# The context recurrence's gate products, done per head in half the array's rows instead of in block-diagonal pairs

## The chip, the cores and the metric

One core of a Trainium2 chip. The time is device microseconds of one whole execution. TensorE (PE) multiplies, VectorE (DVE) and ScalarE (ACT) work elementwise and bring results out of the eight PSUM banks, SyncE (SP) issues the transfers. Each engine takes its own instructions in the order in which they are written, and waits on semaphores for the others.

## The reference, cut to the part that matters

The program is a transformer block followed by a mixer block. The mixer's recurrence (RG-LRU) starts from states that 256 context tokens give. For them, in both directions n:

```python
def rglru(v, lp, h0):
    xc = jnp.stack([depthwise_conv(v, lp['a_conv'][0], A_CONV - 1, 0),
                    depthwise_conv(v, lp['a_conv'][1], 0, A_CONV - 1)])
    xh = xc.reshape(2, bsz, t, N_HEADS_A, HEAD_DIM)                       # 8 heads of 64
    r = jax.nn.sigmoid(jnp.einsum('nbthi,nhij->nbthj', xh, lp['a_wr'])... + lp['a_br'])
    ig = jax.nn.sigmoid(jnp.einsum('nbthi,nhij->nbthj', xh, lp['a_wi'])... + lp['a_bi'])
    log_a = -RG_C * r * jax.nn.softplus(-lp['a_lam'])
    a = jnp.exp(log_a)
    b = jnp.sqrt(-jnp.expm1(2.0 * log_a)) * (ig * xc)
    ...   # h = a * h + b along the tokens; the last h is the mixer's start
```

A head's 64 channels meet a 64x64 matrix of their own for each of the two gates r and ig. The rest of the program is attention, a state space branch, two feed-forward blocks, an embedding and the mixer proper.

## The kernel before

Everything is laid out with channels on the 128 partitions. The context's 512 recurrence channels are four tiles `ct` of 128, that is of two heads each; `KX[n][:, ct]` (128x256) holds the convolved context of direction n, `KR` and `KG` of the same shape take the gates r and ig.

All the orders are written out by hand. One Python function per engine and stage writes that engine's instructions; `tensor` calls, in this order, `glu()`, `context_rows()` (the context's projection), `ssm_rows(0)`, `context_gates()`, `ssm_rows(1)`, `ssm_rows(2)`, `ssm_rows(3)` and then `attention()`. So the context's small products stand between the large products of the state space branch's output (`ssm_rows`, four units of four results `yb`, each result twelve matmuls).

PSUM banks go round: `banks.take(use, end)` gives the next of the eight banks and notes the event that frees it; TensorE waits for the end of the use before. Results `cgt` take sixteen banks in a row, and are freed by ScalarE; results `yb` are freed by VectorE's product with `GBR` into `TMP`.

**TensorE, `context_gates` (L957).** For each ct, n and gate q one product of `GWC[:, ct, 2n+q]` (128x128, the two heads' 64x64 matrices on its diagonal, zeros beside them) and `KX[n][:, ct]`: sixteen products of 256 columns in single precision, each of which the trace shows as two records.

**ScalarE, `context` (L1719).** After a weight conversion (`WS<-RAW`) it takes sixteen sigmoids 128x256 out of the banks, with the gate's bias column; then `CKV<-LR` twice, a table load, four exponentials and four tanh for each direction, then the next weight conversion, three `CQ<-LR`, a table load, two square roots, a weight conversion.

**VectorE, `context` (L2955).** `KG = KG * KX` for each direction waits for ScalarE's last gate of that direction (L2978); then `CKV` twice, four `TMP<-PS,GBR` of `ssm_rows(1)`, the low half of a weight conversion (it waits for ScalarE's high half), six steps on `KR` and `KX`, four `TMP<-PS,GBR` of `ssm_rows(2)`, a weight conversion, `KG*KR` twice, three `CQ`, the eight scans with two copies, four `TMP<-PS,GBR` of `ssm_rows(3)`, and on to the attention's heads.

**The attention's start.** TensorE's first head products (`PS<-CKV,WS`) take banks that are long free; the next (`PS<-WS,CKV`, 24 matmuls) take banks that the `yb` results of `ssm_rows(3)` lie in, and so wait for VectorE's `TMP<-PS,GBR`.

**SyncE** loads GWC once (L3777), long ahead. The mixer proper later does its own gates (`gates`, L1165 and L1985) from a tile `GW` that holds both gates of a head side by side, in products of 64 rows.

Of the kernel before, what the change touches and what calls it, by code (L numbers as in the profile page):

```python
# [7 lines left out]
F32 = mybir.dt.float32  # L8
# [244 lines left out]
def build(nc, t, plan):  # L253
# [28 lines left out]
    def at(name, kb, shape, dt):  # L282
        return nc.alloc_sbuf_tensor_at(name, shape, dt, offset=base + int(kb * KB))
# [46 lines left out]
    ZG = at("ZG", 128, [128, 2, 4, 1024], F32R)  # L330
    CX = at("CX", 184, [128, 8, 256], F32)
    VK = at("VK", 96, [128, 4, 264], F32)
    GWC = at("GWC", 112, [128, 4, 4, 128], F32)
    KX, KR, KG = ([at(f"{name}{n}", 56 + 4 * j + 12 * n, [128, 4, 256], F32) for n in range(2)]
                  for j, name in enumerate(("KX", "KR", "KG")))
    GBR = at("GBR", 80, [128, 2, 1024], F32)
# [121 lines left out]
    def bank(*use):  # L458
        return PS[:, banks.slot.get(use, 0), :]
# [98 lines left out]
    def tensor(e):  # L558
# [9 lines left out]
        def mms(items):  # L568
            for out, l, r, first, last in items:
                done = d.matmul(out, l, r, start=first, stop=last)  # L570
            return done
# [385 lines left out]
        def context_gates():  # L957
            for ct in range(4):
                for n in range(2):
                    for q in range(2):  # L960
                        use = ("cgt", ct, n, q)
                        banks.take(use, (ac, *use))
                        e.wait_ge(dma("gwc")("gwc"), ve("kx", n, ct), *banks.free(use))
                        mms([(bank(*use)[:, 0:256], GWC[:, ct, 2 * n + q, :], KX[n][:, ct], True, True)]).then_inc(*mm.inc(*use))

        def ssm_rows(j):
            u = w.take()
# [380 lines left out]
    def scalar(e):  # L1348
        d, w, side = e.do, Units(forms), iter(())

        def act(out, x, f, bias=0.0, scale=1.0):
            return d.activation(out, x, f, bias=bias, scale=scale)  # L1352
# [366 lines left out]
        def context():  # L1719
            def split(name, dst, i0, n):  # L1720
                for k in range(n):
                    e.wait_ge(dma(f"lr{i0 + k}")("lr"), ve("kx", 1, 3), mm("cgt", 3, 1, 1))
                    if name == "q":
                        e.wait_ge(ve("ckv", 1))
                    act(dst[:, 0, k, :], LR[i0 + k][:], ACT.Copy).then_inc(*ac.inc("c" + name, k))

            for ct in range(4):
                u = w.take()
                e.wait_ge(mm("vk", ct))
                act(VK[:, ct, 3:259], bank("vk", ct)[:, 0:256], ACT.Copy).then_inc(*ac.inc("vk", ct))  # L1730
                release(u)
            ssm_rows(0)
            for ct in range(4):
                for n in range(2):
                    for q, (dst, name) in enumerate(((KR, "a_br"), (KG, "a_bi"))):
                        e.wait_ge(mm("cgt", ct, n, q), mm("glu", 3, 1))
                        act(dst[n][:, ct], bank("cgt", ct, n, q)[:, 0:256], ACT.Sigmoid, bias=col(name, 4 * n + ct)).then_inc(
                            *ac.inc("cgt", ct, n, q))
            split("kv", CKV, 1, 2)
            for n in range(2):  # L1740
                for ct in range(4):
                    e.wait_ge(ve("kg", n))
                    act(KX[n][:, ct], KR[n][:, ct], ACT.Exp, scale=GL[:, 4 * n + ct:4 * n + ct + 1]).then_inc(*ac.inc("kexp", n, ct))
                for ct in range(4):
                    e.wait_ge(ac("kexp", n, 3))
                    act(KR[n][:, ct], KR[n][:, ct], ACT.Tanh, scale=GL[:, 8 + 4 * n + ct:8 + 4 * n + ct + 1]).then_inc(
                        *ac.inc("ktanh", n, ct))
            ssm_rows(1)
            split("q", CQ, 3, 3)
            for n in range(2):  # L1750
                e.wait_ge(ve("kv3", n))
                act(KR[n][:], KR[n][:], ACT.Sqrt, scale=-1.0).then_inc(*ac.inc("ksq", n))
            ssm_rows(2)
            ssm_rows(3)
# [477 lines left out]
    def vector(e):  # L2232
# [722 lines left out]
        def context():  # L2955
# [19 lines left out]
                release(u)  # L2975
            ssm_rows(0)
            for n in range(2):
                e.wait_ge(ac("cgt", 3, n, 1), mm("cgt", 3, n, 1))  # L2978
                tt(KG[n][:], KG[n][:], KX[n][:], ALU.mult).then_inc(*ve.inc("kg", n))
            split("kv", CKV, 1, 2)  # L2980
            ssm_rows(1)
# [667 lines left out]
    def sync(e):  # L3649
# [124 lines left out]
        e.wait_ge(dma("lat")("q"), mm("zt", 3, 1), mm("gb", 7, 1))  # L3774
        load_latent(0)
        d.dma_start(CS0[64:128, :], t["rope"]).then_inc(*dma("cs0").inc("cs"))
        d.dma_start(GWC[:], t["gw"].rearrange("c p (a n) -> p c a n", a=4)).then_inc(*dma("gwc").inc("gwc"))  # L3777
        for i in (1, 2, 3):
            load_latent(i)
        e.wait_ge(mm("glu", 3, 1))  # L3780
# [195 lines left out]
def pack(i):  # L3976
# [58 lines left out]
    for n in ("c_ln_g", "c_ln_b", "c_pw_b", "d_scale"):  # L4035
        c[n] = cols_of(i[n + "_2"][0])
    c["d_b"] = i["d_b_2"][0].T
    gw, gq = np.zeros((4, 128, 4, 128), np.float32), np.zeros((4, 128, 3, 128), np.float32)
    for ct in range(4):
        for n in range(2):  # L4040
            for q, name in enumerate(("a_wr_2", "a_wi_2")):
                for e in range(2):
                    gw[ct, 64 * e:64 * e + 64, 2 * n + q, 64 * e:64 * e + 64] = i[name][0, n, 2 * ct + e]
                    o = 64 * (e ^ q)
                    gq[ct, 64 * e:64 * e + 64, n, o:o + 64] = i[name][0, n, 2 * ct + e]
        gq[ct, :, 2] = i["d_w_2"][0, ct]
# [28 lines left out]
    for a, kind in w:  # L4075
# [5 lines left out]
            tiles.append(a)  # L4081
            entries.append((kind, "ring", (n,), 0))
    arrays = {
        "gw": gw.reshape(4, 128, 512),
        "gq": gq.reshape(4, 128, 384),
        "cnt": np.tile(cnt.reshape(1, 320), (128, 1)),
        "ctxT": i["ctx_2"][0].T.reshape(8, 128, 256),
# [27 lines left out]
```

## Time and profile before

| | us |
|---|---|
| median of 3 runs (lowest to highest) | 3148.76 (3148.34 to 3150.01) |
| time of the profiled execution | 3148.84 |
| its span in the trace | 3147.0 |
| TensorE busy / VectorE busy / ScalarE busy | 3099.2 / 2360.8 / 1254.2 |
| the sixteen context gate products on TensorE | 1144.74 to 1151.46 |
| the sixteen sigmoids on ScalarE, up to the next instruction | 1145.96 to 1152.22 |

Times inside the execution count from the span's start. The stage that the change touches lies at about 1145 to 1152 of 3147. In a timeline, a row is a run of like instructions on one engine: start, length up to the end of the last, and in brackets how long the engine had been idle and what ended the wait. The granted clock is given as a share of TensorE's full clock.

### The profile page before, as it was taken

How to read it: one execution, taken by the hardware profiler on the slowest of the kernel's cores; microseconds unless marked ns; L12 is line 12 of the kernel's file. 1: busy time of each engine (PE TensorE's matmuls, PEld its weight loads, DVE VectorE, ACT ScalarE, POOL GpSimd, SP SyncE). 2: the span in 40 equal slices, each digit the busy share in tenths (PEclk: the TensorE clock that was granted, in tenths of full speed). 3: DMA queues.
4: the chain of work that ended last, by engine and by line, in shares of the span. 5: the costliest groups of instructions: out<-in, count | busy, mean ns of one | idle time of the engine just before them, and what ended most of it. 6: DMA issues, size and time to landing. Idle time of an engine off the chain costs nothing.

```text
span 3147.0 us, 38018 instructions
## 1 busy us (share of the span) xinstructions
PE 3099.2 (98%) x14840; PEld 2531.3 (80%) x14840; DVE 2360.8 (75%) x4053; ACT 1254.2 (40%) x1952; POOL 90.2 (3%) x113
## 2 busy tenths in 40 slices
PE   8999999999999999999999999999999999999998
PEld 6887888877988888888878888888777688788887
DVE  6777767778859678778598767667798689789736
ACT  4233323335242456656243223223365534534414
POOL 0000000000000002332000000000000000000000
PEclk9999999999999999999999999999999999999999
DMA  3222212213333450003211111111111311122242
GB/s 131 74 74 76 78 61 67 68 67 128 104 95 134 142 192 26 14 21 137 99 54 55 53 54 53 54 47 54 67 54 52 114 70 70 41 76 101 80 167 74
DMA packets 89249, 250.15 MB, mean 79 GB/s; under 512 B 8560, under 2 KB 24816, under 8 KB 87536
## 3 DMA queue, kind: packets, MB, share of 16 engines
q1 hardware_dynamic: 89072, 247.73, 22.8%
q8 instruction: 119, 1.95, 0.2%
q14 instruction: 58, 0.48, 0.0%
HBM read 203.65 MB, written 44.04 MB: 79 GB/s over the span
## 4 chain that ended last, share of the span: by engine, by line
PE 90%; DVE 6%; ACT 3%; issue 1%; DMA 0%; POOL 0%; DVEq 0%; SPq 0%; POOLq 0%; ACTq 0%
PE PS L570 88%; PE PS L575 2%; DVE X L2245 1%; DVE WS L2237 1%; DVE XS L2245 1%; DVE HELD L2299 1%; DVE X L2237 1%; ACT XS L1352 0%; DVE XSf L2237 0%; ACT XSf L1352 0%; DMA RAW<-in_W 0%; ACT WS L1352 0%; ACT TMP L1352 0%; DVE TMP L2237 0%; DVE HELD L2237 0%
## 5 line engine op out<-in xcount | busy, mean ns | idle before, releaser
L570 PE MATMUL PS<-XS,WS 128*128 128x512 f32 (+1 forms) x6480 | 1512.2, 390 | 20.6 <-DVE XS L2237 9.4
L570 PEld LDWEIGHTS PS<-XS,WS 128*128 128x128 f32 x6480 | 1207.5, 188 | 297.8 <-issue 26.9
L570 PE MATMUL PS<-HS,WS 128*128 128x512 f32 x2208 | 512.6, 391 | 3.1 <-DVE TMP L2237 2.7
L570 PEld LDWEIGHTS PS<-HS,WS 128*128 128x128 f32 x2208 | 415.2, 188 | 93.6 <-DVE TMP L2237 3.5
L2237 DVE TENSOR_TENSOR WS<-RAW,WS 128x512 fp32r<-128x512 f32 (+1 forms) x398 | 347.2, 881 | 173.1 <-ACT WS L1352 172.5
L1352 ACT ACTIVATE WS<-RAW 128x512 fp32r<-128x512 f32 (+1 forms) x398 | 307.7, 779 | 401.2 <-PE PS L570 350.1
L2237 DVE TENSOR_TENSOR X<-PS,X 128x512 f32<-128x512 f32 x272 | 184.3, 689 | 101.7 <-PE PS L570 101.7
L2237 DVE TENSOR_TENSOR TMP<-TMP,PS 128x512 f32<-128x512 f32 x304 | 203.7, 683 | 61.2 <-PE PS L570 58.4
L570 PE MATMUL PS<-T,WS 128*128 128x512 f32 x960 | 230.6, 389 | 0.0
L570 PEld LDWEIGHTS PS<-T,WS 128*128 128x128 f32 x960 | 180.2, 188 | 37.4
L1352 ACT ACTIVATE TMP<-PS 128x512 f32<-128x512 f32 x144 | 85.0, 596 | 290.5 <-PE PS L570 273.8
L2245 DVE SCALAR_TENSOR_TENSOR CV<-UU,COL,CV 128x1024 f32<-128x1024 f32 x120 | 154.0, 1284 | 3.4
L1352 ACT ACTIVATE HS<-TMP 128x512 fp32r<-128x512 f32 x88 | 55.6, 632 | 211.4 <-DVE TMP L2245 197.2
L2237 DVE TENSOR_TENSOR PT<-PS,PT 128x512 fp32r<-128x512 f32 x128 | 81.7, 679 | 33.7 <-ACT PT L1352 32.3
L570 PE MATMUL PS<-T1h_ln,WS 128*128 128x512 f32 x320 | 105.0, 389 | 0.0
L570 PE MATMUL PS<-KH,QH 128*128 128x512 f32 x384 | 104.1, 406 | 0.2 <-DVE QH L2237 0.2
L1352 ACT ACTIVATE PT<-PS 128x512 fp32r<-128x512 f32 x128 | 69.5, 595 | 59.0 <-PE PS L575 57.7
L1352 ACT ACTIVATE TMP<-TMP 128x512 f32<-128x512 f32 x80 | 50.6, 632 | 101.4 <-DVE TMP L2237 101.4
L2237 DVE TENSOR_TENSOR HS<-TMP,HS 128x512 fp32r<-128x512 f32 x88 | 60.6, 689 | 32.4 <-ACT HS L1352 32.2
L570 PE MATMUL PS<-MH,WS 128*128 128x512 f32 x256 | 80.4, 393 | 0.0
L3050 DVE TENSOR_REDUCE COLB<-PS 128x1 f32<-128x1024 f32 x64 | 77.8, 1215 | 0.4
L1352 ACT ACT_TABLE_LOAD x56 | 71.8, 1283 | 15.1 <-DVE GG L2237 10.7
(337 smaller groups left out, 3663.6 us busy)
## 6 DMA issues: line engine op xcount, KB each, us to landing
RAW<-in_W SPq DMA_DIRECT2D x263, 512.0 KB, 3.3
RAWX<-in_W SPq DMA_DIRECT2D x30, 512.0 KB, 3.2
DC<-TMP SPq DMA_DIRECT2D x32, 256.0 KB, 2.1
X<-in_xT SPq DMA_DIRECT2D x8, 512.0 KB, 8.7
DX<-X SPq DMA_DIRECT2D x2, 2048.0 KB, 9.1
DCZ<-CA SPq DMA_DIRECT2D x8, 512.0 KB, 4.3
DGA<-TMP SPq DMA_DIRECT2D x16, 256.0 KB, 2.1
DGB<-TMP SPq DMA_DIRECT2D x16, 256.0 KB, 2.8
```

The source lines that it names most:

```text
L570: done = d.matmul(out, l, r, start=first, stop=last)
L575: done = d.transpose(out, x, idn)
L1352: return d.activation(out, x, f, bias=bias, scale=scale)
L2237: return d.tensor_tensor(out, a, b, op)
L2245: return d.scalar_tensor_tensor(out=out, in0=a, scalar=s, in1=b, op0=op0, op1=op1)
L2299: d.reciprocal(out[:, 0:width], tmp("rs", name, h)[:, 0:width]).then_inc(*ve.inc("rs", name, h))
L3050: d.tensor_reduce(mx, PS[:, 2 + 2 * (n % 2):4 + 2 * (n % 2), :], AX.XY, ALU.max).then_inc(*ve.inc("mx", n))
```

## The change

The weights of the gates now come from the array that the mixer proper uses: for a head e of tile ct, its 64 rows hold both 64x64 matrices side by side, r's at columns 64e and ig's at columns 64(1-e). A product takes 64 rows (one head, p) and gives both gates of that head as 128 rows of a bank. There are still sixteen products of 256 columns. ScalarE now takes each bank in two quarters of 64x256, and each (ct, n) pair of banks in the order r of p=0, r of p=1, ig of p=0, ig of p=1; ig comes from the other 64 rows of the bank than those that it goes to. A bank is free after its ig quarter. The old array `gw` is gone, and GWC is half as large.

```diff
-    GWC = at("GWC", 112, [128, 4, 4, 128], F32)
+    GWC = at("GWC", 112, [128, 4, 2, 128], F32)
...
             for ct in range(4):
                 for n in range(2):
-                    for q in range(2):
-                        use = ("cgt", ct, n, q)
-                        banks.take(use, (ac, *use))
+                    for p in range(2):
+                        use, rows = ("cgt", ct, n, p), slice(64 * p, 64 * p + 64)
+                        banks.take(use, (ac, "cgi", ct, n, p))
                         e.wait_ge(dma("gwc")("gwc"), ve("kx", n, ct), *banks.free(use))
-                        mms([(bank(*use)[:, 0:256], GWC[:, ct, 2 * n + q, :], KX[n][:, ct], True, True)]).then_inc(*mm.inc(*use))
+                        mms([(bank(*use)[:, 0:256], GWC[rows, ct, n, :], KX[n][rows, ct], True, True)]).then_inc(*mm.inc(*use))
...
-                    for q, (dst, name) in enumerate(((KR, "a_br"), (KG, "a_bi"))):
-                        e.wait_ge(mm("cgt", ct, n, q), mm("glu", 3, 1))
-                        act(dst[n][:, ct], bank("cgt", ct, n, q)[:, 0:256], ACT.Sigmoid, bias=col(name, 4 * n + ct)).then_inc(
-                            *ac.inc("cgt", ct, n, q))
+                    for what, dst, name in (("cgr", KR, "a_br"), ("cgi", KG, "a_bi")):
+                        for p in range(2):
+                            rows, at_ = slice(64 * p, 64 * p + 64), 64 * p if what == "cgr" else 64 - 64 * p
+                            e.wait_ge(mm("cgt", ct, n, p), mm("glu", 3, 1))
+                            act(dst[n][rows, ct], bank("cgt", ct, n, p)[at_:at_ + 64, 0:256], ACT.Sigmoid,
+                                bias=col(name, 4 * n + ct)[rows]).then_inc(*ac.inc(what, ct, n, p))
...
-                e.wait_ge(ac("cgt", 3, n, 1), mm("cgt", 3, n, 1))
+                e.wait_ge(ac("cgi", 3, n, 1), mm("cgt", 3, n, 1))
...
-        d.dma_start(GWC[:], t["gw"].rearrange("c p (a n) -> p c a n", a=4)).then_inc(*dma("gwc").inc("gwc"))
+        d.dma_start(GWC[:], t["gq"].rearrange("c p (a n) -> p c a n", a=3)[:, :, 0:2]).then_inc(*dma("gwc").inc("gwc"))
```

ScalarE's order at the gates of tile ct = 0, before (`KR_109`, `KG_111` are r and ig of direction 0, `KR_110`, `KG_112` of direction 1):

```order
L1352 ACTIVATE WS<-RAW 128x1024 [waits matmul_done,dma_unit1]
L1352 ACTIVATE KR_109<-PS,COL 128x256 [waits matmul_done]
L1352 ACTIVATE KG_111<-PS,COL 128x256 [waits matmul_done]
L1352 ACTIVATE KR_110<-PS,COL 128x256 [waits matmul_done]
L1352 ACTIVATE KG_112<-PS,COL 128x256 [waits matmul_done]
```

And the same place now:

```order
L1352 ACTIVATE WS<-RAW 128x1024 [waits matmul_done,dma_unit1]
L1352 ACTIVATE KR_109<-PS,COL 64x256 [waits matmul_done] x2
L1352 ACTIVATE KG_111<-PS,COL 64x256 x2
L1352 ACTIVATE KR_110<-PS,COL 64x256 [waits matmul_done] x2
L1352 ACTIVATE KG_112<-PS,COL 64x256 x2
```

Sixteen instructions of 128 rows have become thirty-two of 64 rows; nothing else on ScalarE has another place.

TensorE's order from the last four gate products into `ssm_rows(1)`, which reads the same in both kernels, since only the rows of the operands differ (`KX_107`, `KX_108` are the two directions):

```order
L570 MATMUL PS<-KX_107,GWC 128x256 [waits activation_done] x2
L570 MATMUL PS<-KX_108,GWC 128x256 [waits activation_done] x2
L570 MATMUL PS<-ZG,WS 128x512 [waits activation_done,weight_lo_done,weight_hi_done]
L570 MATMUL PS<-ZG,WS 128x512 x11
L570 MATMUL PS<-ZG,WS 128x512 [waits activation_done]
```

The first eight gate products take banks that older results held; the last eight each wait for ScalarE to free one of the first eight's, and the eight results of `ssm_rows(1)` and `ssm_rows(2)` each for one of the last eight's. The event they wait for has moved to the ig quarter of that bank.

VectorE's order behind the gates, which also reads the same in both:

```order
L2237 TENSOR_TENSOR WS<-RAW,WS 128x1024 [waits weight_hi_done]
L2237 TENSOR_TENSOR KG_111<-KG_111,KX_107 128x1024 [waits matmul_done,activation_done]
L2237 TENSOR_TENSOR KG_112<-KG_112,KX_108 128x1024 [waits matmul_done,activation_done]
L2237 TENSOR_TENSOR CKV<-LR_115,CKV 128x1024 [waits activation_done]
L2237 TENSOR_TENSOR CKV<-LR_116,CKV 128x1024 [waits activation_done]
L2237 TENSOR_TENSOR TMP<-PS,GBR 128x512 [waits dma_gbr0,matmul_done]
```

The wait of `KG_112` has moved from the sixteenth full sigmoid to the thirty-second quarter, that of `KG_111` from the fourteenth to the twenty-eighth.

## Rows read from the trace of the kernel before

**Rows 1.** the page: busy us, share and count by engine; chain by engine

```profile
PE 3099.2 (98%) x14840; PEld 2531.3 (80%) x14840; DVE 2360.8 (75%) x4053; ACT 1254.2 (40%) x1952; POOL 90.2 (3%) x113
...
PE 90%; DVE 6%; ACT 3%; issue 1%; DMA 0%; POOL 0%; DVEq 0%; SPq 0%; POOLq 0%; ACTq 0%
```

**Rows 2.** timeline of TensorE, 1136 to 1215: start, length, instruction, [idle before, releaser]

```profile
1144.74 7.07 PE L570 MATMUL PS<-KX,GWC 128*128 128x256 f32 x32
1151.46 33.00 PE L570 MATMUL PS<-ZG,WS 128*128 128x512 f32 x144
1184.30 2.88 PE L570 MATMUL PS<-CKV,WS 128*128 128x512 f32 x12
1187.55 3.10 PE L570 MATMUL PS<-WS,CKV 128*128 128x256 f32 x24 [0.37 <-DVE TMP L2237]
1191.06 4.34 PE L570 MATMUL PS<-CQ,WS 128*128 128x512 f32 x18 [0.42 <-DVE KH L2237]
...
1198.50 2.98 PE L570 MATMUL PS<-KH,QH 128*128 128x512 f32 x12 [0.22 <-DVE QH L2237]
```

**Rows 3.** timeline of ScalarE in the same stretch, same columns

```profile
1145.96 0.46 ACT L1352 ACTIVATE KR<-PS,COL 128x256 f32<-128x256 f32 x1
1146.32 0.46 ACT L1352 ACTIVATE KG<-PS,COL 128x256 f32<-128x256 f32 x1
...
1151.84 0.48 ACT L1352 ACTIVATE KG<-PS,COL 128x256 f32<-128x256 f32 x1
1152.22 2.00 ACT L1352 ACTIVATE CKV<-LR 128x1024 fp32r<-128x1024 f32 x2
...
1160.62 1.71 ACT L1352 ACTIVATE KR<-KR,COLB 128x256 f32<-128x256 f32 x4
1162.80 1.06 ACT L1352 ACTIVATE WS<-RAW 128x1024 fp32r<-128x1024 f32 x1 [0.47 <-PE PS L570]
```

**Rows 4.** timeline of VectorE in the same stretch (TENSOR_TENSOR and others)

```profile
1151.49 2.36 DVE L2237 TENSOR_TENSOR KG<-KG,KX 128x1024 f32<-128x1024 f32 x2 [4.11 <-ACT KG L1352]
...
1163.89 1.23 DVE L2237 TENSOR_TENSOR WS<-RAW,WS 128x1024 fp32r<-128x1024 f32 x1 [0.46 <-ACT WS L1352]
...
1171.28 1.88 DVE L2237 TENSOR_TENSOR TMP<-PS,GBR 128x512 f32<-128x512 f32 x3
1173.62 0.69 DVE L2237 TENSOR_TENSOR TMP<-PS,GBR 128x512 f32<-128x512 f32 x1 [0.46 <-PE PS L570]
1174.77 1.23 DVE L2237 TENSOR_TENSOR WS<-RAW,WS 128x1024 fp32r<-128x1024 f32 x1 [0.46 <-ACT WS L1352]
...
1186.71 2.48 DVE L2237 TENSOR_TENSOR TMP<-PS,GBR 128x512 f32<-128x512 f32 x4
```

**Rows 5.** timeline of ScalarE, 2570 to 2620: the mixer's gates in quarters

```profile
2590.87 2.81 ACT L1352 ACTIVATE GG<-PS,COL 64x512 f32<-64x512 f32 x4
```

**Rows 6.** groups by line and form: busy us, mean ns

```profile
L1352 ACT ACTIVATE GG<-PS,COL 64x512 f32<-64x512 f32 x32 | 21.9, 685 | 0.8
```

**Rows 7.** timeline of TensorE, 2570 to 2620: the mixer's half-array pairs

```profile
2589.62 1.99 PE L570 MATMUL PS<-XC,GW 64*128 64x512 f32 x8
2591.54 22.05 PE L570 MATMUL PS<-XS,WS 128*128 128x512 f32 x96
```

**Rows 8.** timeline of TensorE, 1120 to 1145

```profile
1132.11 12.79 PE L570 MATMUL PS<-ZG,WS 128*128 128x512 f32 x48 [2.36 <-issue]
```

**Rows 9.** 2 us windows: busy PE, PEld, DVE, ACT, POOL; then clock, DMA share, GB/s

```profile
1132.00:1134.00 2.00, 1.89 (x8) 1.56 (x9) 1.89 (x6) 1.01 (x1) 0.00 (x0) 0.89 0.62 231
1134.00:1136.00 2.00, 2.00 (x6) 1.63 (x5) 1.89 (x5) 0.92 (x2) 0.00 (x0) 0.50 0.23 88
1136.00:1138.00 2.00, 2.00 (x8) 1.55 (x8) 1.93 (x4) 0.19 (x1) 0.00 (x0) 0.75 0.18 25
```

**Rows 10.** the tile GWC: its load and how long it took to land

```profile
L3777 SPq DMA_DIRECT2D GWC<-in_gw x1: 587/587/587, 1091.9 to 1091.9; - x1
...
DMA to landing us min/median/max: 8.8/8.8/8.8
```

More of the change, by code:

```diff
@@ L4037, in pack @@
     c["d_b"] = i["d_b_2"][0].T
-    gw, gq = np.zeros((4, 128, 4, 128), np.float32), np.zeros((4, 128, 3, 128), np.float32)
+    gq = np.zeros((4, 128, 3, 128), np.float32)
     for ct in range(4):
@@ L4042, in pack @@
                 for e in range(2):
-                    gw[ct, 64 * e:64 * e + 64, 2 * n + q, 64 * e:64 * e + 64] = i[name][0, n, 2 * ct + e]
                     o = 64 * (e ^ q)
@@ L4083, in pack @@
     arrays = {
-        "gw": gw.reshape(4, 128, 512),
         "gq": gq.reshape(4, 128, 384),
```

## The prediction

> **What bounds the kernel now.** I read the page first: TensorE is busy for 98% of the span, and the chain that ended last is 90% TensorE and 6% VectorE [rows 1]. So a change matters if it moves TensorE, or if it moves one of the few places where TensorE waits. Then the timeline of TensorE around the change: the gate products start at 1144.74, the next instruction at 1151.46, so the sixteen products hold TensorE for 6.72 us, 0.42 each; then come twelve `yb` results without a gap until 1184.30, the first head products until 1187.18 (1184.30 + 2.88), a wait of 0.37 us for VectorE's `TMP`, and smaller waits of 0.42 and 0.22 us up to the scores at 1198.50 [rows 2]. The first of these waits says that at 1187 VectorE, not TensorE, is last. What VectorE does before it is in its own timeline: four short waits (4.11, 0.46, 0.46, 0.46 us), and none from 1174.77 to 1186.71, a full queue [rows 4]. Its longest, 4.11 us, is for ScalarE's gates. ScalarE's timeline: sixteen sigmoids from 1145.96 to 1152.22, 6.26 us, then work without a gap up to a wait of 0.47 us at 1162.80 [rows 3]. So the chain to watch is ScalarE's gates, its work up to `WS<-RAW`, VectorE's queue, `TMP` at 1186.71, TensorE at 1187.55.
>
> **TensorE's products.** The same number of instructions and columns, on 64 rows instead of 128. The trace has this form in the mixer: eight records of 64x512 start at 2589.62, the next instruction at 2591.54, 1.92 us [rows 7]. A record of 256 columns holds TensorE for 0.21 us (6.72/32), one of 512 columns for twice that, 0.42; eight in sequence would be 3.4 us, four 1.7. So two heads do run beside each other, and the context's products would take 6.72/2 = 3.4 us if nothing held them: a gain of 3.3 us at the most.
>
> **ScalarE's quarters.** Here is the cost: 32 instructions for 16, each of as many columns. A full sigmoid lasts 0.46 to 0.48 us, but in a queue the next starts 0.36 us after it (1146.32 - 1145.96): they overlap by 0.1 [rows 3]. The mixer's quarters, which alternate between the halves of the rows as the new ones do, do not: four last 2.81 us [rows 5] at 0.685 each [rows 6], so they start (2.81 - 0.685)/3 = 0.71 us apart, 0.02 more than one lasts. I take the same for 256 columns: 0.47 + 0.02 = 0.49 us apart. The bounds: below, 0.36 apart, if they overlap as the full ones do; above, the mixer's 0.71, for twice the columns. I take the length from the row with the same 256 columns and the missing overlap from the row with the same order of halves, the same bias column and the same PSUM source. Sum: 32 x 0.49 = 15.7 us instead of 6.26, ScalarE is 9.4 us late behind the gates (5.3 at 0.36; 16.5 at 0.71, which only a quarter whose length does not depend on its columns would give).
>
> The Trainium skill, "ScalarE: Activation LUTs", section "What ACT_TABLE_LOAD costs", gives an activation with a bias column about 280 ns + 0.833 ns a column and says that back-to-back ones overlap by about 93 ns; that makes an estimate of 0.40 us apart, 12.8 us for 32. The mixer's rows agree with its duration (0.707 against 0.685) and not with the overlap where the halves alternate.
>
> **TensorE behind the gates.** Its pairs no longer wait for TensorE's own pace but for banks. The first eight products find theirs free; product 8 (the ninth) needs the ig quarter of product 0, and so on. The first `yb` of `ssm_rows(1)` takes the bank of the ninth product, whose ig quarter is the nineteenth of ScalarE's: 1145.96 + 19 x 0.49 = 1155.3, against 1151.46 before. So TensorE, instead of gaining 3.3 us, is 3.8 us late here, and arrives at the wait of 1187.55 at 1187.18 + 3.8 = 1191.0. What counts is when VectorE arrives there.
>
> **VectorE's queue.** ScalarE's lag of 9.4 reaches its `WS<-RAW` less the gap before it: tanh ended at 1160.62 + 1.71 = 1162.33 and the conversion could start 0.09 earlier, by the overlap of queued rows, instead of 1162.80 [rows 3]. That gives back 0.56: the conversion is 8.8 us late. VectorE's low half waits for it (the 0.46 at 1163.89 says so) and is 8.8 late too, 1172.7; slack that VectorE has before it doesn't help, because this wait comes behind it. From there VectorE runs in a full queue to 1171.28, now 1180.1. The fourth `TMP` no longer waits for TensorE (the 0.46 at 1173.62, with a 0.08 overlap: 0.54 back), nor the conversion behind it for ScalarE (0.46 at 1174.77, again 0.54) [rows 4]; ScalarE's own one can start once the second square root is done, 1180.2 + 1.0, and ends at 1182.3, VectorE asks for it at 1182.6. What is left is 8.85 - 1.08 = 7.8 us. `TMP` of 1186.71 starts at 1194.5, TensorE's 1187.55 becomes 1195.3. TensorE has arrived 4.3 us before. **TensorE is 7.8 us late from here on**, and so is all that it feeds.
>
> **Other edits.** GWC is loaded half as large and at the same place of SyncE's queue; it was issued at 1091.9 and landed 8.8 us later, 44 us before its use [rows 10]: nothing, and without that cover at most those few us. VectorE's `KG` waits for another count, costed above. SyncE's loads for the `yb` products are issued behind the `TMP` results of two rows earlier and move with them.
>
> **The clock.** Before `ssm_rows(0)` TensorE was idle for 2.36 us [rows 8], and in the 2 us windows behind it the granted clock is 0.89, 0.50 and 0.75 of full [rows 9]: from 2.4 to 1.2 GHz and back. What is lost at full clock is (0.11 + 0.50 + 0.25) x 2 = 1.7 us. The new wait before 1195.3 is 4.3 us of idleness, longer than that one, so I expect the clock to fall there too. TensorE has 0.42 + 0.22 = 0.64 us of slack up to the scores [rows 2]: cost 1.7 - 0.64, about 1.0 us; bounds 0 (it does not fall) and about 3 (twice the loss, if it stays down for longer). It will likely fall among the gates as well; there TensorE is not last and it costs nothing.
>
> **The sum.** 3148.84 (the profiled execution's own time, 0.08 above the median, which I leave at that) + 7.8 + 1.0 = 3157.6 us. Behind the scores TensorE is bound by its own work again, so I take nothing off; waits for transfers are 0% of the chain [rows 1].
>
> The Trainium skill, "TensorEngine Tiling (Array Packing)", section "PSUM Bottleneck", speaks against the change: "Tiling speeds up TensorE but not PSUM evacuation". It puts no price on it; the price here is the 9.4 us of the rows.
>
> **The rivals.**
> A. The forecast: quarters 0.47 to 0.51 apart. ScalarE +8.8 to +10.1, lag 7.1 to 8.5, clock 0 to 3: 3156 to 3160. Chance 0.78. For it: the mixer's rows, the same code with other sizes.
> B. The other side, not slower by what can be measured: the quarters overlap, 0.36 to 0.41 apart. ScalarE +5.3 to +6.9, lag 3.6 to 5.2, no clock loss up to the full 1.0: 3152.4 to 3155.0. It decides at a spacing of (6.3 - 1.0 + 1.64 + 6.26)/32 = 0.41 us with the clock's 1.0, 0.44 without: below that the change is not slower by 0.2%. For it: the full sigmoids' 0.36; against it: the mixer's rows [rows 5, 6]. Chance 0.16. The overlap that the Trainium skill states in "ScalarE: Activation LUTs", section "What ACT_TABLE_LOAD costs", would lead here, with 0.40.
> C. TensorE's gain comes through: 3148.8 - 3.3 = 3145.5. It needs ScalarE's lag to vanish into slack before 1187, and the wait of 0.37 there says that there is none; TensorE would have to be last, and even then its own banks hold it. Chance 0.03.
> D. The halves do not run side by side here, although they do in the mixer: TensorE takes 6.7 us as before. Then nothing changes in the sum, since ScalarE sets the pace. It has no time of its own and lies in A and B.
> E. Something behind adds to it (quarters longer than the full sigmoids, or a longer stretch at half clock): above 3160.5, chance 0.03.
>
> **How the numbers follow.** The likeliest case gives 3157.6. The range from 3152.8 to 3160.5 takes in A with both bounds of the clock and most of B. A measurement of this kernel can tell about 0.2%, 6.3 us, from no change: slower by more than that means above 3155.1. A and E, less its lowest corner: 0.77; within: B and that corner, 0.20; faster: C, 0.03.
>
> **What would show it.** ScalarE's `KR` and `KG` rows as 64x256, 32 of them, 0.49 apart, up to about 1161.7; if 0.36 to 0.40 apart, B. TensorE's first `yb` row behind the gates at 1155.3, with waits for ScalarE among the `KX,GWC` rows. VectorE's wait for `KG` grown from 4.1 to about 12 us. `TMP` at 1194.5 and behind it TensorE's row at 1195.3 with a wait of about 4 us for `TMP`. The granted clock below 1 in windows among the gates and behind 1195. The forecast is wrong if VectorE arrives at `TMP` with less lag than 6 us, or if TensorE's waits further behind shrink in return.

## The result and the profile after

| | median | lowest to highest | runs |
|---|---|---|---|
| before | 3148.56 us | 3147.21 to 3150.22 | 8 |
| after the change | 3156.9 us | 3156.45 to 3160.17 | 8 |

The ratio is 1.0028, with a 95% interval of 1.0018 to 1.0038: the change makes the kernel 8.3 us slower, forecast were 8.8. The profiled execution of the changed kernel took 3160.17 us, the longest of its eight; its span is 3158.4 us, and part of what it has over the median lies outside the changed stage (below).

The page after it, the lines that answer to [rows 1] (busy us, share and count by engine; the chain's walk back covers only 64% of the span here, so its shares are not compared):

```profile
span 3158.4 us, 38034 instructions
...
PE 3107.5 (98%) x14840; PEld 2535.2 (80%) x14840; DVE 2360.2 (75%) x4053; ACT 1263.1 (40%) x1968; POOL 90.4 (3%) x113
```

ScalarE has sixteen instructions more and is busy for 9 us more; VectorE's work is the same.

TensorE's timeline, 1130 to 1225, which answers to [rows 2]:

```profile
1144.48 1.13 PE L570 MATMUL PS<-KX,GWC 64*128 64x256 f32 x8
1145.88 2.40 PE L570 MATMUL PS<-KX,GWC 64*128 64x256 f32 x8 [0.27 <-DVE TMP L2239]
1148.54 1.19 PE L570 MATMUL PS<-KX,GWC 64*128 64x256 f32 x4 [0.26 <-ACT KG L1352]
1150.52 1.71 PE L570 MATMUL PS<-KX,GWC 64*128 64x256 f32 x4 [0.79 <-ACT KG L1352]
...
1156.55 34.49 PE L570 MATMUL PS<-ZG,WS 128*128 128x512 f32 x144 [0.37 <-ACT KG L1352]
1190.88 2.88 PE L570 MATMUL PS<-CKV,WS 128*128 128x512 f32 x12
1196.52 4.60 PE L570 MATMUL PS<-WS,CKV 128*128 128x256 f32 x24 [2.76 <-DVE TMP L2239]
1200.96 4.25 PE L570 MATMUL PS<-CQ,WS 128*128 128x512 f32 x18
...
1207.92 2.91 PE L570 MATMUL PS<-KH,QH 128*128 128x512 f32 x12
```

The first four products (eight records) take 1.13 us, side by side; four full ones took 4 x 0.42 = 1.7. The next four wait for banks that VectorE's `TMP` frees. From the ninth on TensorE waits for ScalarE's ig quarters, as the rows `<-ACT KG` say, and the `yb` products start 12.1 us behind the first gate product (1156.55 - 1144.48), where it was 6.7. And before the second group of head products TensorE waits 2.76 us for VectorE's `TMP`.

ScalarE's timeline in the same stretch, which answers to [rows 3]:

```profile
1147.04 0.95 ACT L1352 ACTIVATE KR<-PS,COL 64x256 f32<-64x256 f32 x2
1148.02 0.96 ACT L1352 ACTIVATE KG<-PS,COL 64x256 f32<-64x256 f32 x2
...
1161.88 0.97 ACT L1352 ACTIVATE KG<-PS,COL 64x256 f32<-64x256 f32 x2
1162.88 2.02 ACT L1352 ACTIVATE CKV<-LR 128x1024 fp32r<-128x1024 f32 x2
...
1172.90 1.04 ACT L1352 ACTIVATE WS<-RAW 128x1024 fp32r<-128x1024 f32 x1
```

Thirty-two quarters from 1147.04 to 1162.88: 15.84 us, 0.495 apart (0.49 was forecast), and 0.469 is the middle length of a `KR` quarter. `WS<-RAW` has no wait before it any more.

VectorE's timeline, which answers to [rows 4]:

```profile
1160.90 1.23 DVE L2239 TENSOR_TENSOR KG<-KG,KX 128x1024 f32<-128x1024 f32 x1 [12.24 <-ACT KG L1352]
1162.88 1.23 DVE L2239 TENSOR_TENSOR KG<-KG,KX 128x1024 f32<-128x1024 f32 x1 [0.76 <-ACT KG L1352]
...
1173.98 1.23 DVE L2239 TENSOR_TENSOR WS<-RAW,WS 128x1024 fp32r<-128x1024 f32 x1 [3.97 <-ACT WS L1352]
...
1181.37 2.48 DVE L2239 TENSOR_TENSOR TMP<-PS,GBR 128x512 f32<-128x512 f32 x4
1183.76 1.21 DVE L2239 TENSOR_TENSOR WS<-RAW,WS 128x1024 fp32r<-128x1024 f32 x1
...
1195.68 2.48 DVE L2239 TENSOR_TENSOR TMP<-PS,GBR 128x512 f32<-128x512 f32 x4
```

The wait for `KG` has grown from 4.11 to 12.24 us; behind the wait for `WS` at 1173.98 the queue is full up to `TMP`, and the two waits of 0.46 that stood there are gone. The kernel before also had three waits of VectorE for `yb` results ahead of `WS` (0.58, 2.03 and 2.03 us, from 1156 to 1163), which [rows 4] leaves out; now one of 1.15 us is left of them, at 1169.32.

**Measuring by events.** Two executions reach this stage at times up to 1.7 us apart (the first sigmoid at 1145.96 before, 1147.04 after), so I compare distances between events of one execution: from the start of the first `KR<-PS` to that of the last row `TMP<-PS,GBR`, and from there to the first score (`KH,QH`). The column "ScalarE" is the time from the first sigmoid to `CKV`. All times in us, from the timelines; "waits" is TensorE's before `WS,CKV`.

| kernel | ScalarE | sigmoid to TMP | waits | TMP to score | sigmoid to score |
|---|---|---|---|---|---|
| before | 6.26 | 40.75 | 0.37 | 11.79 | 52.54 |
| after | 15.84 | 48.64 | 2.76 | 12.24 | 60.88 |
| e1_quarters | 15.79 | 48.60 | 4.83 | 12.76 | 61.36 |
| e2_grouped | 13.52 | 46.45 | 0.37 | 11.79 | 58.24 |
| e3_tiles64 | 5.70 | 39.74 | 0.37 | 11.78 | 51.52 |
| e4_noscan | 15.79 | 43.63 | none | 13.44 | 57.07 |
| e5_fill_head | 15.79 | 48.61 | 0.16 | 11.79 | 60.40 |
| e6_noscan_fill | 15.87 | 43.70 | none | 11.79 | 55.49 |
| e7_half | 10.77 | 43.57 | 2.29 | 11.79 | 55.36 |
| e8_fill_both | 15.80 | 48.62 | 1.62 | 11.79 | 60.41 |
| e9_grouped_fill | 13.55 | 46.36 | none | 11.80 | 58.16 |
| e10_change (the changed kernel again) | 15.82 | 48.63 | 1.97 | 11.78 | 60.41 |
| e11_grouped (e2_grouped again) | 13.55 | 47.38 | 0.37 | 11.80 | 59.18 |

In the two profiled executions the difference of the spans, 11.4 us, falls into three parts: 1.08 ahead of the first sigmoid, 8.34 from there to the first score, and 2.0 behind it (1948.5 us from the first score to the end before, 1950.5 after). In the outer two both kernels do the same, and the clock fell once more often in each of them in the changed kernel's execution: ahead of the stage at 754 and 1095 (before: at 1133.6), behind it at 1484. The tail shows what such a fall costs. All executions have a fall in their last 20 us. In the seven profiled ones without another behind the first score (before, e2, e3, e4, e6, e9, e10) the rest takes 1948.5 to 1948.7 us, whatever the kernel; in the five with one 1949.8 to 1950.5, in e7_half with two 1951.9.

### The profile page after: what moved, and what is told of

The parts are those of the page before. It is cut to its first block, busy times and chain, and to the rows that moved or that the text cites. A ratio compares the mean times of both kernels' runs of the same rounds, so it can differ in the third digit from the quotient of the medians.

```text
span 3158.4 us, 38034 instructions
## 1 busy us (share of the span) xinstructions
PE 3107.5 (98%) x14840; PEld 2535.2 (80%) x14840; DVE 2360.2 (75%) x4053; ACT 1263.1 (40%) x1968; POOL 90.4 (3%) x113
## 4 chain that ended last, share of the span: by engine, by line
PE 55%; DVE 5%; ACT 3%; issue 1%; DMA 0%; POOL 0%; DVEq 0%; POOLq 0%; ACTq 0%; SPq 0%
PE PS L570 54%; PE PS L575 2%; DVE WS L2239 1%; DVE HELD L2301 0%; DVE X L2239 0%; DVE X L2247 0%; DVE KX L2247 0%; DVE XS L2247 0%; ACT KR L1352 0%; DVE TMP L2239 0%; ACT XS L1352 0%; DVE XSf L2239 0%; ACT KG L1352 0%; DVE TMP L2247 0%; ACT L1352 0%
## 5 line engine op out<-in xcount | busy, mean ns | idle before, releaser
L3052 DVE TENSOR_REDUCE COLB<-PS 128x1 f32<-128x1024 f32 x64 | 77.8, 1215 | 0.5
```

Source lines behind the costliest of these rows:

```text
L3052: d.tensor_reduce(mx, PS[:, 2 + 2 * (n % 2):4 + 2 * (n % 2), :], AX.XY, ALU.max).then_inc(*ve.inc("mx", n))
```

## The experiments

All changes are against the changed kernel, unless it says otherwise. e1 to e4 shared a chip with runs of the kernel before, whose median was 3148.62 us there; for e5 to e8 it was 3148.57, for e9 to e11 3148.43. A ratio's interval of 0.001 to each side is 3 us. So the intervals do not separate kernels whose medians are one or two us apart; where I compare such kernels, the argument rests on the distances in the traces, of one execution each.

### e1_quarters: the quarters alone

```diff
 # against the kernel before
                     for q, (dst, name) in enumerate(((KR, "a_br"), (KG, "a_bi"))):
-                        e.wait_ge(mm("cgt", ct, n, q), mm("glu", 3, 1))
-                        act(dst[n][:, ct], bank("cgt", ct, n, q)[:, 0:256], ACT.Sigmoid, ...)
+                        for p in range(2):
+                            rows = slice(64 * p, 64 * p + 64)
+                            e.wait_ge(mm("cgt", ct, n, q), mm("glu", 3, 1))
+                            act(dst[n][rows, ct], bank("cgt", ct, n, q)[rows, 0:256], ACT.Sigmoid, ...)
```

> The kernel before with one part of the change alone: TensorE's sixteen full products stay, ScalarE takes each bank in two quarters of 64x256 instead of one sigmoid of 128x256. My theory (ScalarE's 32 quarters, 0.49 us apart because the halves of the rows alternate, set the end): the quarters take 15.8 us as in the changed kernel, VectorE's TMP before the head products comes 7.5 to 9 us late, and the time is that of the changed kernel within 1 us, 3156 to 3158 us. Rival 1 (the half-array products or the order of their banks are what costs): about 3148.6 us. Rival 2 (it costs more than in the changed kernel, since TensorE also keeps its 3.3 us): 3160 us.

Measured: 3158.9 us (3157.26 to 3160.27, 6 runs), ratio 1.0031 (1.0019 to 1.0042). ScalarE 15.79 us, `TMP` at 48.60: as in the changed kernel to 0.05 us, without any half-array product. Rival 1 falls: the quarters alone make the whole lag at `TMP`, without the new products, rows and banks. Rival 2 (3160 us) has the median almost as near as my range has, but not its mechanism: TensorE's first `yb` starts 8.99 us behind the first sigmoid (9.51 in the changed kernel), and TensorE waits 4.83 us for `TMP`, so it is not last. The median is 0.9 us above the range of my theory; 0.5 of it is the longer way from `TMP` to the score (12.76), behind a wait of 4.83 us, and the rest I can't tell from the spread of the runs.

### e2_grouped: another order of the quarters

```diff
 # the events that free the banks and release KG follow the new order
+                for what, dst, name, p in (("cgr", KR, "a_br", 0), ("cgi", KG, "a_bi", 1), ("cgr", KR, "a_br", 1), ("cgi", KG, "a_bi", 0)):
+                    for n in range(2):
```

> The changed kernel with ScalarE's quarters in another order: for each tile both directions' r of head 0, then both ig of head 1 (same rows of PSUM, other rows of SBUF), both r of head 1 (other rows of PSUM, same of SBUF), both ig of head 0. Every second quarter uses the same rows as the one before it. My theory (a quarter cannot overlap the one before it if it changes the half of the rows): 16 starts 0.36 us and 16 starts 0.49 us behind the one before, 13.6 us in all instead of 15.8, and the time falls by about 2.2 us, to 3154.5 us. Rival (a quarter of 64 rows never overlaps, whatever comes before it): 0.49 everywhere, time as the changed kernel, 3157 us. The trace also tells whether a change of the PSUM rows alone or of the SBUF rows alone is enough.

Measured: 3157.47 us (3154.51 to 3158.46, 10 runs), ratio 1.0027 (1.0018 to 1.0037). ScalarE's timeline, in which each row is two quarters on the same rows:

```profile
1148.44 0.83 ACT L1352 ACTIVATE KR<-PS,COL 64x256 f32<-64x256 f32 x2
1149.30 0.83 ACT L1352 ACTIVATE KG<-PS,COL 64x256 f32<-64x256 f32 x2
1150.15 0.83 ACT L1352 ACTIVATE KR<-PS,COL 64x256 f32<-64x256 f32 x2
1151.01 0.82 ACT L1352 ACTIVATE KG<-PS,COL 64x256 f32<-64x256 f32 x2
```

A row lasts 0.83, and a quarter 0.46, so the second starts 0.36 behind the first; the next row starts 0.49 behind that (0.855 from row to row). So 64 rows do overlap, as full ones do, if the one before used the same half, and the rival falls. From a `KR` row to a `KG` row the half of SBUF changes (with the bias column's) and that of PSUM doesn't, from `KG` to `KR` it is the other way round: either alone costs the overlap. (The tile changes too from `KR` to `KG`, but the full sigmoids alternate in the same way and overlap.) `TMP` came 2.19 us earlier (46.45), as forecast. But the median is 3157.47 and not 3154.5, no better than the changed kernel's. Two things could hide the 2.2 us: what happens elsewhere in the execution, or TensorE. Its banks come free later in this order (the first `yb` starts 9.98 us behind the first sigmoid, 9.51 in the changed kernel), its clock is halved for ten us there, and it takes 34.22 us for the `yb` products. The next three runs are on that.

### e9_grouped_fill, e10_change, e11_grouped: where the reordering's 2.2 us went

e10_change is the changed kernel, e11_grouped is e2_grouped, and e9_grouped_fill is e2_grouped with this:

```diff
-                        mms([(bank(*use)[:, 0:256], GWC[rows, ct, n, :], KX[n][rows, ct], True, True)]).then_inc(*mm.inc(*use))
+                        mms([(bank(*use)[:, 0:256], GWC[rows, ct, n, :], KX[n][rows, ct], True, True)] * 3).then_inc(*mm.inc(*use))
...
+                if p == 0:
+                    mms(group3(PS[:, m, :], pairs))
                 mms(group3(PS[:, m, :], pairs)).then_inc(*mm.inc(*use))
```

> e2_grouped with TensorE's gate products issued three times and the first two head products twice, as in e8_fill_both. In e2_grouped the first score came 2.64 us earlier than in the changed kernel's profile, but the median time did not fall. My theory: in e2_grouped TensorE, at half clock among the gates, arrives together with VectorE at the head products, so that in many executions it is last; with the clock kept up this goes: from the first sigmoid to the first score 58.2 us, and the median 2 us or more below that of the changed kernel on the same chip. Rival: the medians of e2_grouped and the changed kernel differ by what happens elsewhere, and the filling changes nothing: this kernel within 0.5 us of e2_grouped.

> The changed kernel itself, for comparison on one chip with the two others of this call. All theories: 3156.5 to 3158 us, 48.6 us from the first sigmoid to TMP.

> e2_grouped again, beside the changed kernel on one chip. My theory: its median is 0.5 to 2 us below the changed kernel's, less than the 2.2 us by which TMP comes earlier, since TensorE is then as late as VectorE. Rival (the order of the quarters gains nothing at all): the same median as the changed kernel within 0.5 us.

Measured on one chip: e10_change 3157.54 us (3156.32 to 3158.65, 8 runs), ratio 1.0027 (1.0017 to 1.0037); e11_grouped 3156.99 us (3155.39 to 3158.41, 10 runs), ratio 1.0027 (1.0018 to 1.0037); e9_grouped_fill 3155.42 us (3154.02 to 3157.68, 11 runs), ratio 1.0022 (1.0013 to 1.0031). TensorE's timeline of e11_grouped:

```profile
1155.70 35.12 PE L570 MATMUL PS<-ZG,WS 128*128 128x512 f32 x144 [1.44 <-ACT KG L1352]
```

and of e9_grouped_fill:

```profile
1156.43 32.93 PE L570 MATMUL PS<-ZG,WS 128*128 128x512 f32 x144
```

With the clock kept up the reordering is worth 2.1 us in the median and 2.25 in the stage (58.16 against 60.41, which e8_fill_both, the changed kernel with the same filling, needs too); without it, 0.55 in the median and 1.2 in the stage. So TensorE at half clock had taken part of the gain: in e11_grouped VectorE's `TMP` is itself late (47.38), since the `yb` results come late (VectorE waits 0.38 us for one and then 0.46 for ScalarE's `WS`, and in e9_grouped_fill for neither). The intervals of the three overlap, and 0.55 lies so near the rival's 0.5 that the medians do not separate the two; it is the stage's times in the traces that tell the cause. They do not explain all: in e2_grouped's own profiled execution the stage had gained 2.64 us, in spite of the fall, and the median had not. Even so, ScalarE's rearranged quarters with the filling are 7 us slower than the kernel before.

### e3_tiles64: one gate of both heads in one bank

```diff
 # against the kernel before, with the changed kernel's weights
+                        for p in range(2):
+                            rows, o = slice(64 * p, 64 * p + 64), 64 * (p ^ q)
+                            items.append((bank(*use)[rows, 0:256], GWC[rows, ct, n, o:o + 64], KX[n][rows, ct], True, True))
```

> The changed kernel's weights, but each product split into 64 rows by 64 columns of the array, so that a bank holds one gate of both heads and ScalarE again takes sixteen full sigmoids of 128x256; 32 products instead of 16. My theory: two tiles with other rows and other columns run beside each other, TensorE's products take some 3.4 us instead of 6.7 if the banks let them, ScalarE 0.36 apart takes 5.8 us instead of 6.3; VectorE, which is last at the head products, comes only 0.5 to 2 us earlier: 3146.5 to 3148.3 us. Rival (tiles of 64x64 run one after another): TensorE holds 6.7 us or more for them and the time is that of the kernel before, 3148.6 us, or up to 3 us more.

Measured: 3149.27 us (3147.25 to 3151.18, 11 runs), ratio 1.0001 (0.9992 to 1.001): no change that can be measured. TensorE's timeline:

```profile
1143.14 7.21 PE L570 MATMUL PS<-KX,GWC 64*64 64x256 f32 x64
1150.28 32.93 PE L570 MATMUL PS<-ZG,WS 128*128 128x512 f32 x144
```

Sixty-four records in 7.14 us: 0.11 each, so two do run beside each other. My 3.4 us was wrong: I had halved the time of the sixteen products and forgotten that there are now thirty-two. Two at a time they need as long as before. With ScalarE at 0.36 apart `TMP` comes 1.0 us earlier, as forecast, and so does the first score, but the medians don't show it: 3149.27 lies above my 3146.5 to 3148.3 and where the rival had it, though the rival's reason (one tile after another) is not what the trace shows. It also says that ScalarE's full tiles, given back, take away the whole loss.

### e4_noscan: VectorE's queue shortened

```diff
-                for ct in range(4):
-                    y, x, b = (v[n][:, ct, ::-1] if n else v[n][:, ct] for v in (KR, KX, KG))
-                    scan(y, x, b, 0.0).then_inc(*ve.inc("kscan", n, ct))
```

> The changed kernel without VectorE's eight context scans (4.9 us of its queue between the gates and the TMP results that the head products wait for); the part left out is the recurrence over the context tokens, the final states are taken from what the tiles hold. My theory (VectorE's queue is last there, TensorE arrives 3 to 4.3 us before it): TMP comes 4.9 us earlier, TensorE's wait goes, the clock does not fall there, and the time falls by 3.5 to 5.5 us, to 3151.5 to 3153.5 us; 3.8 us of TensorE's own lag from the gates stay. Rival (TensorE's own stalls among the gates make the loss): the time stays at 3157 us.

Measured: 3155.21 us (3153.34 to 3157.14, 10 runs), ratio 1.0019 (1.001 to 1.0029); the profiled execution took 3153.34. `TMP` came 5.0 us earlier (43.63), TensorE's wait is gone, and the first score came 3.81 us earlier. So VectorE was last in the changed kernel, and TensorE's own lag is next behind it. The way from `TMP` to the score is 13.44 us, 1.65 more than before: TensorE starts `WS,CKV` 3.59 us behind `TMP`, where VectorE would let it start after 0.84, and makes up 1.1 of these 2.75 us because it has no waits any more (9.85 us from there to the score, 10.95 before). The stage's 3.81 us lie in the forecast of 3.5 to 5.5; the median fell by 1.7 only. The profiled execution is the fastest of the ten, and where the other 2.1 us of the median went its trace doesn't show. The clock, in 2 us windows of e4_noscan (busy PE, PEld, DVE, ACT, POOL; then granted clock):

```profile
1148.00:1150.00 2.00, 1.21 (x6) 0.62 (x5) 0.00 (x0) 1.90 (x5) 0.00 (x0) 1.00 1.07 272
1150.00:1152.00 2.00, 1.63 (x6) 0.91 (x5) 0.00 (x0) 1.90 (x5) 0.00 (x0) 0.51 0.90 285
...
1158.00:1160.00 2.00, 2.00 (x6) 1.52 (x6) 0.24 (x1) 1.90 (x5) 0.00 (x0) 0.50 0.00 0
1160.00:1162.00 2.00, 2.00 (x10) 1.62 (x9) 1.24 (x2) 1.90 (x5) 0.00 (x0) 0.93 0.02 4
```

Behind the first gates, where TensorE is busy for 1.21 of 2 us and on half of its rows, the clock is 1.2 GHz for ten us, almost five of them in `yb` products (from 1155.43 on), whose twelve then take 35.2 us instead of 32.9.

### e6_noscan_fill: the same with TensorE kept busy among the gates

```diff
 # against e4_noscan
-                        mms([(bank(*use)[:, 0:256], GWC[rows, ct, n, :], KX[n][rows, ct], True, True)]).then_inc(*mm.inc(*use))
+                        mms([(bank(*use)[:, 0:256], GWC[rows, ct, n, :], KX[n][rows, ct], True, True)] * 3).then_inc(*mm.inc(*use))
```

> The kernel of e4_noscan (no context scans) with each of TensorE's context gate products issued three times, the last one counting. In e4_noscan TensorE was last at the head products, and its granted clock was 0.5 from 1150 to 1160. My theory: the clock fell because TensorE had too little to do among the gates, and that cost e4_noscan what VectorE's earlier arrival had gained; with the filling the clock stays at 1, the twelve yb results take 33 us instead of 35, and the time falls by 1.5 to 2 us against e4_noscan's 3155.2, to about 3153.4 us. Rival: the clock falls in the same way (it is not a matter of how busy TensorE is), and the time stays or grows.

Measured: 3152.74 us (3151.09 to 3154.25, 11 runs), ratio 1.0012 (1.0004 to 1.0021), 2.5 us below e4_noscan. TensorE's timeline:

```profile
1145.04 11.19 PE L570 MATMUL PS<-KX,GWC 64*128 64x256 f32 x96
1156.19 32.92 PE L570 MATMUL PS<-ZG,WS 128*128 128x512 f32 x144
```

Three times the work, no fall of the clock among the gates, `yb` in 32.92 us, the first score 1.58 us earlier than in e4_noscan. The clock fell because TensorE had too little to do, and where TensorE is last that costs 1.6 us. The medians' 2.5 us are more than the 1.5 to 2 forecast and more than the stage shows; the two ran on different chips and their intervals overlap.

### e5_fill_head and e8_fill_both: what the clock costs the changed kernel

```diff
+                if p == 0:
+                    mms(group3(PS[:, m, :], pairs))
                 mms(group3(PS[:, m, :], pairs)).then_inc(*mm.inc(*use))
```

> The changed kernel with TensorE's first two head products issued twice (the second time they start the sum anew, the result is the same): 2.9 us of work in the time in which TensorE waits for VectorE's TMP. My theory of the clock: without the long wait the granted clock does not fall behind the head products' wait, and from the first of the four TMP results to the first score it takes the 11.8 us of the kernel before instead of 12.2 to 12.8; TMP itself comes at the same time; total 0.4 to 1.0 us less than the changed kernel, which is near what the runs can resolve. Rival: the clock falls there anyway, or falls without a cost: no change; or TensorE becomes last with the added work, up to 0.5 us more.

> The changed kernel with both fillings: gate products three times, first head products twice. My theory: no fall of the clock from 1145 to 1210; TMP still 48.6 us behind the first sigmoid, since ScalarE and VectorE set it; first score 11.8 to 12.2 us behind TMP; total within 1 us of e5_fill_head. So the clock's fall among the gates costs the changed kernel nothing there. Rival (part of the loss is TensorE at half clock among the gates): 1.5 to 2 us less than e5_fill_head.

Measured: e5_fill_head 3156.96 us (3156.68 to 3158.4, 9 runs), ratio 1.0026 (1.0016 to 1.0036); e8_fill_both, with e6's tripled gate products as well, 3157.79 us (3157.07 to 3159.1, 6 runs), ratio 1.0028 (1.0017 to 1.0039). In both `TMP` is where it was, 48.6, and from `TMP` to the score it takes 11.79 us, as before the change. The changed kernel's own windows there:

```profile
1194.00:1196.00 2.00, 0.00 (x0) 0.00 (x0) 1.97 (x5) 0.00 (x0) 0.00 (x0) 1.00 0.00 0
1196.00:1198.00 2.00, 1.48 (x10) 1.51 (x11) 2.00 (x4) 0.00 (x0) 0.00 (x0) 0.86 0.40 147
1198.00:1200.00 2.00, 2.00 (x12) 2.00 (x11) 1.90 (x3) 1.70 (x3) 0.00 (x0) 0.50 0.90 221
1200.00:1202.00 2.00, 2.00 (x11) 1.83 (x11) 1.30 (x3) 1.95 (x5) 0.00 (x0) 0.79 1.07 371
```

So the fall behind the wait is there, it is brought about by the wait, and it costs 12.24 - 11.79 = 0.45 us in this execution (0.97 in e1_quarters, where the wait is 4.83 us). In e10_change, the same kernel in another execution, the wait was 1.97 us, no fall followed, and the way to the score took 11.78: the term is there in some executions and not in others. The time does not show such an amount: the changed kernel's medians are 3156.9 and 3157.54 us, e5_fill_head's is 3156.96 and not 0.4 to 1.0 less, e8_fill_both's 3157.79. That e8 is no faster than e5 fits the other part: among the gates the fall costs the changed kernel nothing, since TensorE has a wait of 2.76 us to give. Where that wait is gone, as in e11_grouped and e4_noscan, it costs. (In e5 and e8 the clock stayed up behind a wait of 0.16 and 1.62 us.)

### e7_half: half the dose

```diff
 # against e1_quarters
-                        for p in range(2):
-                            rows = slice(64 * p, 64 * p + 64)
+                        for p in range(2 - q):
+                            rows = slice(64 * p, 64 * p + 64) if q == 0 else slice(0, 128)
```

> As e1_quarters (full products), but only r is taken in quarters, ig in one full sigmoid: 16 quarters and 8 full ones. By the rows: 16 x 0.49 + 8 x 0.36 to 0.43 = 10.8 to 11.3 us on ScalarE, 4.5 to 5 us more than before. My theory says that the first 1.64 us of such a lag disappear in gaps before VectorE's queue is full, and the rest reaches TensorE one to one: from the first sigmoid to TMP 43.7 to 44.2 us (40.75 before, 48.6 with 32 quarters), total 3151.5 to 3152.5 us with no fall of the clock. Rival (the loss is in proportion to ScalarE's extra time, 7.9 of 9.5): TMP at 44.5 to 45 us, total 3152.5 to 3153.5.

Measured: 3152.36 us (3151.59 to 3155.25, 11 runs), ratio 1.0013 (1.0004 to 1.0022). ScalarE took 10.77 us, 4.51 more than before; `TMP` stood at 43.57, 2.82 more; both lie just under their ranges, and the median is in mine. The clock fell neither among the gates nor behind the wait of 2.29 us. The 1.64 us of gaps that the prediction took off give 4.51 - 1.64 = 2.87; in proportion (7.89 of 9.58) it would be 3.7. With the full dose: 9.58 - 1.64 = 7.94, measured 7.89. Between them, in e2_grouped, ScalarE took 7.26 us more than before: 7.26 - 1.64 = 5.62, measured 5.70. The gaps are eaten first, then it is one to one. The medians alone could not have told this from the proportion; the distance to `TMP` does.

## Why the prediction was right

**TensorE's products.** Two heads side by side, and no gain, because banks hold them: both right. The stall was put at 3.8 us of lag; measured from the first sigmoid, the first `yb` comes 9.51 us behind it (1156.55 - 1147.04) against 5.50 before, 4.0 us of lag.

**ScalarE's quarters.** 0.49 us forecast, 0.495 measured; +9.4 forecast, +9.58 measured. This was the term that decided, and that it was not 0.40 or less hung on the mixer's rows alone. The full sigmoids were partly held by TensorE themselves (0.36 us apart up to the ninth, 0.43 from there on, against its 0.42 a product); the 6.26 us count both, so the sum is not touched. e2_grouped shows what is behind it, a change of half in either memory. The rule of the Trainium skill ("ScalarE: Activation LUTs", section "What ACT_TABLE_LOAD costs") that back-to-back activations overlap holds here for quarters on the same rows (0.46 long, 0.36 apart, about the 93 ns it states) and not for those that change the half (0.469 long, 0.495 apart).

**VectorE's queue.** Lag 7.8 forecast, 7.89 measured; e4_noscan shows that it is what TensorE waits for, e7_half that the gaps add up as worked out. The waits of the trace, 12.24 us for `KG` and those that vanished, are the forecast's. I had counted four waits of VectorE in the kernel before and overlooked three for `yb` results, of 0.58, 2.03 and 2.03 us. They lie ahead of the wait for `WS`, which comes last, so the sum stands as it is.

**The clock.** Behind the wait for `TMP` it fell in one profiled execution of the changed kernel and not in the other (e10_change). Its price was 0.45 us and nothing, where I put 1.0: this term of the sum was two or more times too large, within its bounds. One reason is the slack up to the scores, which I had as 0.64 us from TensorE's idle times; e4_noscan, without waits there, shows 1.1 (9.85 us instead of 10.95), and 1.7 - 1.1 would have been 0.6. The wait was 2.76 us and not 4.3, because TensorE itself was slower: I let the fall among the gates cost nothing, which is true for the end, but it took 1.5 us of TensorE's slack (`yb` in 34.49 us instead of 33.0). And that the clock fell behind the wait at all was in part luck, because waits of this size do not bring a fall each time. Ahead of `ssm_rows(0)` TensorE was idle for 2.33 to 2.51 us in eight of the thirteen profiled executions; the clock fell behind it in five (12.8 us for the `yb` row, as in [rows 8]) and not in three (e1, e3 and e7), of which e3_tiles64 shows

```profile
1132.05 11.16 PE L570 MATMUL PS<-ZG,WS 128*128 128x512 f32 x48 [2.39 <-issue]
```

Behind the wait for `TMP` it fell after 4.83 and 2.76 us and not after 2.29, 1.97 and 1.62.

**The sum.** 8.34 us from the first sigmoid to the first score, which is 7.89 + 0.45 (7.87 in e10_change), and 8.3 between the medians. That these agree to 0.1 us is partly chance: beside e10_change, on another chip, the medians lie 9.1 us apart. The forecast's 8.8 is 7.8 and 1.0, the stage's 8.34 is 7.89 and 0.45. Behind the score nothing was given back, as the tails of 1948.5 to 1948.7 us show. Rival B fell with the 0.495 us of the changed kernel's own rows, rival C with TensorE's wait for `TMP`.

"TensorEngine Tiling (Array Packing)", section "PSUM Bottleneck", of the Trainium skill says that tiling speeds up TensorE and not the taking out of PSUM. The traces agree with both parts (the first four products take 1.13 us instead of 1.7) and go further: here taking out got slower, by 9.58 us, for the 3.3 that could have been gained.

What stays open: how much of the spread of a kernel's runs (3.7 us in the changed one) is falls of the clock elsewhere. The profiled executions fit that, by their tails, and so do the mean granted clocks of the changed kernel's eight runs: 0.995 in the two longest, 0.996 or 0.997 in the others. But no run tested it. It is also open why the medians of e2_grouped and e4_noscan gained so much less than their traces. Nor did any version here beat the kernel before by what can be measured.

## What to carry to other kernels

Before splitting a result over more banks or rows, count the instructions that take it out and look up how far apart they start, not how long they last: here splitting each in two doubled that time, and alternating between the halves of the memory added more than a third to it (0.36 to 0.49 us). An engine that is 40% busy can still be the one that sets the end, if its work stands ahead of another engine's full queue; follow the waits in the stage, and take off only the gaps that lie on the chain of last waits. And if an engine is made to wait, look at who gets slower by idling: here TensorE's clock.

## What the runs showed of the hardware

- ScalarE: an activation that reads another half of PSUM's partitions, or writes another half of SBUF's (and takes its bias column from there), than the one before starts 0.02 us after its end; else 0.1 us before its end (64x256: 0.495 and 0.36 apart).
- TensorE's clock among the gates was at half for ten us in all six profiled executions with the half-array products issued once (the changed kernel, e2, e4, e5, e10, e11), although none of TensorE's waits there is longer than 0.79 us in the changed kernel. It stayed up with the same products issued three times (e6, e8, e9), with full products (before, e1, e7) and with 64x64 tiles (e3). The busy time of a window does not tell these apart: in e1_quarters it is 1.42 of 2 us at full clock, in the changed kernel 2.00 and then 1.47 in the windows up to the fall. What does is not tested. Half-array products use half of the rows, but two of them also run in less time than two full ones (a row of 1.19 us in each 1.98 at full clock, against 2 x 0.70 in e1_quarters), so TensorE also had less to do.

In e1_quarters:

```profile
1150.00:1152.00 2.00, 1.42 (x5) 0.59 (x4) 0.00 (x0) 1.90 (x5) 0.00 (x0) 1.00 0.92 331
```

In the changed kernel:

```profile
1146.00:1148.00 2.00, 2.00 (x8) 1.03 (x8) 2.00 (x4) 1.89 (x3) 0.00 (x0) 1.00 0.94 346
1148.00:1150.00 2.00, 1.47 (x6) 0.59 (x4) 0.66 (x1) 1.88 (x5) 0.00 (x0) 0.92 1.04 287
1150.00:1152.00 2.00, 1.48 (x4) 0.99 (x4) 0.00 (x0) 1.90 (x5) 0.00 (x0) 0.50 0.94 201
```

- TensorE's idle time of 2.33 to 2.51 us ahead of `ssm_rows(0)` was followed by a fall of the clock in five executions and by none in three; with the fall the same 48 records took 12.8 us instead of 11.2.
- Tiles of 64x64 in diagonal pairs ran two at a time, 0.11 us a record of 256 columns (e3_tiles64), no faster than tiles of 64x128 (96 records in 11.15 us in e6_noscan_fill). Whether four can run at once in another order was not tried.
